# A decoder layer with 32 experts: expert 0's gather in two column pieces, its bias in the last quarter, and the first input chunk ahead of token tile 1

## The reference, cut to what matters

```python
h = rms_norm(x, norm1_w)                       # x: 256 tokens x 1024
proj = h @ w_in                                # 1024 x 3072: rq rk rv rg mq mk mv
ret  = retention(rotary(rq), rotary(rk), rv)   # 4 heads; group norm, times silu(rg)
moba = causal attention(rotary(mq), rotary(mk), mv)   # 8 heads of 64, one block of 256
x = x + concat(ret, moba) @ w_out
h2 = rms_norm(x, norm2_w)
logits = h2 @ w_router + b_router              # 32 experts, top 4, softmax over the chosen
for e in experts:                              # over the tokens that chose e
    u = h2[tok] @ w1[e] + b1[e]                # 1024 -> 2048: gate and linear halves
    y = clamped_swiglu(u) @ w2[e] + b2[e]      # 1024 -> 1024
    acc[tok] += y * gate
out = rms_norm(x + acc, final_norm_w)
```

## Time and profile before

| | before |
|---|---|
| median of 3 runs | 1040.47 us (1039.09 to 1041.36) |
| profiled execution, in all | 1039.17 us |
| its span, first to last instruction | 1037.3 us |
| TensorE matmuls busy | 1020.7 us, 98% of the span |
| VectorE busy | 245.4 us, 24% |
| ScalarE busy | 126.5 us, 12% |
| read from HBM | 422.78 MB, 409 GB/s over the span |
| granted TensorE clock | 0.997 of full |

### The profile page before, as it was taken

The page is one execution under the profiler, slowest core; times in us unless marked ns, Lnnn a source line. Parts: engine busy times, 40 slices in busy tenths (PEclk is TensorE's granted clock), DMA queues, the critical chain, the costliest instruction groups (busy, mean ns, idle before and its releaser), DMA issues.

```text
span 1037.3 us, 11270 instructions
## 1 busy us (share of the span) xinstructions
PE 1020.7 (98%) x4880; PEld 409.8 (40%) x4880; DVE 245.4 (24%) x610; ACT 126.5 (12%) x246; POOL 0.2 (0%) x4
## 2 busy tenths in 40 slices
PE   9999999999999999999999999999999999999996
PEld 8888433333333333333333333333333333333331
DVE  5776332111111111111111111111111111111111
ACT  2433120000000000000000000000000000000002
POOL 0000000000000000000000000000000000000000
PEclk9999999999999999999999999999999999999999
DMA  9983999999999999999999999999999999999995
GB/s 324 365 337 143 418 376 425 426 428 426 434 432 426 438 429 427 435 427 429 434 429 433 430 428 437 429 428 435 426 432 433 429 430 433 428 436 420 430 421 227
DMA packets 36104, 424.64 MB, mean 409 GB/s; under 512 B 3176, under 2 KB 16112, under 8 KB 19536
## 3 DMA queue, kind: packets, MB, share of 16 engines
q1 hardware_dynamic: 35744, 423.51, 97.0%
q10 hardware_dynamic: 304, 0.33, 0.1%
HBM read 422.78 MB, written 1.05 MB: 409 GB/s over the span
## 4 chain that ended last, share of the span: by engine, by line
PE 90%; DMA 7%; SPq 1%; DVE 0%; another core or an unknown queue 0%; issue 0%; ACT 0%; DVEq 0%
PE PS L1837 40%; PE PS L1860 19%; DMA ring<-in_w 7%; PE PS L1442 6%; PE PS L1806 5%; PE PS L1788 5%; PE PS L1685 3%; PE PS L1645 3%; PE PS L1895 2%; PE PS L1798 2%; PE PS L1411 1%; PE PS L1780 1%; SPq L543 1%; PE PS L1388 0%; PE PS L1968 0%; PE PS L1982 0%
## 5 line engine op out<-in xcount | busy, mean ns | idle before, releaser
L1837 PE MATMUL PS<-ring,work 128*64 128x512 f32 x1976 | 433.8, 596 | 6.0 <-DMA ring<-in_w 5.5
L1837 PEld LDWEIGHTS PS<-ring,work 128*64 128x64 f32 x1976 | 139.6, 137 | 277.2 <-issue 266.5
L1860 PE MATMUL PS<-ring,work 128*64 128x512 f32 x1024 | 227.9, 596 | 0.9 <-DMA ring<-in_w 0.8
L1860 PEld LDWEIGHTS PS<-ring,work 128*64 128x64 f32 x1024 | 72.0, 137 | 153.8 <-issue 148.9
L1300 DVE TENSOR_SCALAR work<-PS 128x512 f32<-128x512 f32 x32 | 22.1, 691 | 385.4 <-PE PS L1837 385.4
L841 ACT ACTIVATE work<-work 128x512 f32<-128x512 f32 x32 | 20.2, 631 | 523.5 <-DVE work L1300 523.5
L1265 DVE TENSOR_TENSOR work<-PS,n2w 128x512 f32<-128x512 f32 x30 | 20.7, 691 | 228.5 <-PE PS L1798 228.5
L1442 PE MATMUL PS<-ring 128*128 128x256 f32 x280 | 64.5, 382 | 0.0
L1806 PE MATMUL PS<-late,work 64*128 64x512 f32 x248 | 61.9, 616 | 0.0
L1788 PE MATMUL PS<-resid,work 128*64 128x512 f32 x248 | 58.5, 592 | 0.0
L1442 PEld LDWEIGHTS PS<-ring 128*128 128x128 f32 x280 | 51.7, 190 | 7.7 <-issue 1.4
(11 more groups left out here) (196 smaller groups left out, 453.2 us busy)
## 6 DMA issues: line engine op xcount, KB each, us to landing
ring<-in_w SPq DMA_DIRECT2D x72, 4096.0 KB, 34.8
ring<-in_w SPq DMA_DIRECT2D x35, 2048.0 KB, 13.5
ring<-in_w SPq DMA_DIRECT2D x22, 1024.0 KB, 8.4
ring<-in_w_in SPq DMA_DIRECT2D x11, 1024.0 KB, 12.1
ring<-in_w_out SPq DMA_DIRECT2D x4, 1024.0 KB, 11.1
ring<-in_w SPq DMA_DIRECT2D x6, 512.0 KB, 7.0
ring<-in_w_in SPq DMA_DIRECT2D x2, 512.0 KB, 5.8
work<-in_w SPq DMA_DIRECT2D x1, 768.0 KB, 8.2
```

The source lines that it names most:

```text
L1837: last = mm(bank(b0 + v)[64 * half:64 * half + 64, :], rows[:, c, :], turned_half(w[:, v * F:(v + 1) * F], half), start=(second and c == 0 ...
L1860: last = mm(out[64 * half:64 * half + 64, :], aT_n[:, c, 64 * h:64 * h + 64], ring[:, 2 * d + c // 2, cols:cols + BANK], start=(h == 0 and ...
```

## The change

- **Start.** The first half of `w_in`'s chunk 0 comes in two pieces (`WIN0_PARTS`, blocks 0 to 1 and 2 to 3), its second half is loaded ahead of x's tile 1 instead of behind it, and `project_first` does seven of tile 0's eight blocks before it transposes tile 1 (`X_TURN_AT`).
- **Projected columns.** `nat` is 1536 columns a tile instead of 3072: three areas of 512 that several chunks use one after the other (`NAT_COL`). With `mixT_moba` it fills slots 16 and 17 alone. Slot 18 and half of slot 19 are free.
- **Loads.** Three quarters of g 9 (`EARLY`, 1.5 MiB) are loaded right behind g 3, the last quarter once `w_in` is used up. The order of g 6, 8, 9, 11 changes. `moved_w` comes in one load of 1 MiB when the logits are done.
- **Expert 0's gather.** It is cut by columns into pieces `a` = 0 and 1 of 256 columns for each half of the partitions, in banks 4 and 7; rows go to `gx1`, outside `moved_w`. Each engine copies two pieces, four full 128 x 128 transposes take the place of the eight small ones, and `gh` is made in four parts, of which the first lets expert 0 begin.
- **Bias.** Expert 0's `b1` is added by the ordinary `bias` ahead of its last quarter (q = 3), its selector made by `make_bsel(0)` on VectorE behind the gather; `make_bsel(1)` moves behind `take_gather(1)`.

The diff, cut to its core:

```diff
-TURN0_BANK = (5, 3)
+ROWS0_BANK, TURN0_BANK = (4, 7), (5, 3)
...
+WIN0_PARTS, X_TURN_AT = [(0, 2), (2, C // 2)], C - 1
...
+AREA_A, AREA_B, AREA_C, NAT_COLS = 0, 512, 1024, 1536
+NAT_COL = [AREA_A, AREA_A + 256, AREA_B, AREA_B + 256, AREA_A, AREA_A + 256, AREA_B, AREA_B + 256,
+           AREA_C, AREA_C + 256, AREA_B, AREA_B + 256]
+NAT_V, NAT_RV, NAT_RG, NAT_RET, NAT_SIG = AREA_A, AREA_C, AREA_B, AREA_C, AREA_A
...
-FIRST_ORDER = [0, 1, 2, 3, 4, 5, 10, 11, 6, 8, 9, 7]
+FIRST_ORDER = [0, 1, 2, 3, 4, 5, 10, 9, 11, 8, 6, 7]
+EARLY, EARLY_COLS = 9, 3 * 1024
...
-        nat_flat = ring[:, HEAD_CHUNKS:HEAD_CHUNKS + 3, :].rearrange("p s n -> p (s n)")
-        nat = nat_flat.rearrange("p (t n) -> p t n", t=T)
-        mixT_moba = ring[:, HEAD_CHUNKS + 3, 0:4 * SEQ].rearrange("p (c n) -> p c n", c=4)
+        nat_flat = ring[:, HEAD_CHUNKS:HEAD_CHUNKS + 2, :].rearrange("p s n -> p (s n)")
+        nat = nat_flat[:, 0:T * NAT_COLS].rearrange("p (t n) -> p t n", t=T)
+        mixT_moba = nat_flat[:, T * NAT_COLS:].rearrange("p (c n) -> p c n", c=4)
...
-            load_win(0, 0, C // 2, win0_in)
+            for n, (c0, c1) in enumerate(WIN0_PARTS):
+                load_win(0, c0, c1, win0_in[n])
+            load_win(0, C // 2, C, head_full[0])
             sp.dma_start(resid[:, 1, :], x_v[:, 1, :]).then_inc(x_in[2], 16)
...
+            early_dst = ring[:, 2 * EARLY:2 * EARLY + 2, :].rearrange("p a n -> p (a n)")
+            early_src = w2_half(0, 1)
...
                 elif g == 8:
                     sp.wait_ge(retT_done, 2)
-                elif g == 9:
-                    sp.wait_ge(retT_done, 2)
                     sp.wait_ge(chunk_used, HEAD_CHUNKS - 2)
+                elif g == EARLY:
+                    sp.wait_ge(chunk_used, WIN_CHUNKS)
                 else:
                     sp.wait_ge(chunk_used, min(2 * g + 2, HEAD_CHUNKS))
...
                     sp.dma_start(ring[:, 2 * d + 1, :], w2_half(1, 1)[:, SLOT_COLS:]).then_inc(ahead_in, 16)
+                    sp.dma_start(early_dst[:, 0:EARLY_COLS], early_src[:, 0:EARLY_COLS]).then_inc(early_part_in, 16)
+                elif g == EARLY:
+                    sp.dma_start(early_dst[:, EARLY_COLS:], early_src[:, EARLY_COLS:]).then_inc(pair_full[EARLY], 16)
...
-            sp.dma_start(moved_w[:, BANK:], moved_src[:, BANK:]).then_inc(moved_in, 16)
-            sp.wait_ge(gather0_done, 2)
-            sp.dma_start(moved_w[:, 0:BANK], moved_src[:, 0:BANK]).then_inc(moved_end_in, 16)
+            sp.dma_start(moved_w, moved_src).then_inc(moved_in, 16)
...
-            act.wait_ge(rows0_done, 1)
-            nc.scalar.activation(gx[0:64, :], bank(4)[0:64, :], ACT.Copy).then_inc(rows0a_ready, 1)
+            for a in range(2):
+                act.wait_ge(rows0_done, a + 1)
+                nc.scalar.activation(gx1[0:64, a * SEQ:(a + 1) * SEQ], bank(ROWS0_BANK[a])[0:64, 0:SEQ],
+                                     ACT.Copy).then_inc(rows0a_ready, 1)
...
-            dve.wait_ge(rows0_done, 2)
-            nc.vector.tensor_copy(gx[64:P, :], bank(4)[64:P, :]).then_inc(rows0b_ready, 1)
-            take_gather0(0).then_inc(gh0_ready, 1)
-            take_gather0(1).then_inc(gh_ready, 1)
-            dve.wait_ge(bias_done, 1)
+            def take_rows0(a):
+                dve.wait_ge(rows0_done, a + 1)
+                nc.vector.tensor_copy(gx1[64:P, a * SEQ:(a + 1) * SEQ],
+                                      bank(ROWS0_BANK[a])[64:P, 0:SEQ]).then_inc(rows0b_ready, 1)
+            def take_gather0(half, a):
+                c = 4 * half + 2 * a
+                return nc.vector.tensor_tensor(gh[:, c:c + 2, :],
+                                               bank(TURN0_BANK[a])[:, 0:2 * P].rearrange("p (c h s) -> p h c s", c=2, h=2)[:, half],
+                                               n2w[:, c:c + 2].unsqueeze(2).broadcast_to([P, 2, SLOTS]), ALU.mult)
+            take_rows0(0)
+            take_rows0(1)
+            dve.wait_ge(gather0_done, 1)
+            take_gather0(0, 0).then_inc(gh0_ready, 1)
+            dve.wait_ge(gather0_done, 2)
+            take_gather0(0, 1).then_inc(gh0_ready, 1)
+            take_gather0(1, 0).then_inc(gh0_ready, 1)
+            take_gather0(1, 1).then_inc(gh_ready, 1)
+            make_bsel(0)
             make_pick(1)
             softmax(0)
             softmax(1)
             link(nc.vector.reduce_max(most[:, :], bank(2)[:, T * E:(T + 1) * E], AX.X))
             nc.vector.tensor_copy(most_i[:, :], most[0:1, :]).then_inc(most_ready, 1)
             take_gather(1)
+            dve.wait_ge(bias_done, 1)
+            make_bsel(1)
             run_experts(dve, expert_dve, 0)
             with dve.If(read["dve"] > SLOTS):
             def project_first():
...
-                pe.wait_ge(win0_in, 16)
                 pe.wait_ge(hT_ready, 1)
-                project_part(0, 0, 0, C // 2)
+                for n, (c0, c1) in enumerate(WIN0_PARTS):
+                    pe.wait_ge(win0_in[n], 16)
+                    project_part(0, 0, c0, c1)
+                pe.wait_ge(head_full[0], 16)
+                pe.wait_ge(hT_ready, 2)
+                project_part(0, 0, C // 2, X_TURN_AT)
                 for half in range(2):
                     transpose_x(1, half)
-                pe.wait_ge(head_full[0], 16)
-                pe.wait_ge(hT_ready, 2)
-                project_part(0, 0, C // 2, C)
+                project_part(0, 0, X_TURN_AT, C)
                 pe.wait_ge(hT_ready, 4)
                 project_part(0, 1, 0, C // 2)
                 pe.wait_ge(ones_ready, 1)
...
+            def gather0_rows(t, a):
+                for half in range(2):
+                    last = mm(bank(ROWS0_BANK[a])[64 * half:64 * half + 64, 0:SEQ], pick[:, t, :],
+                              resid[:, t, half * BANK + a * SEQ:half * BANK + (a + 1) * SEQ],
+                              start=(t == 0), stop=(t == T - 1))
+                return last
+            def turn_rows0(a):
+                gx_v = gx1.rearrange("p (i s) -> p s i", s=DEAL)
+                for s in range(2):
+                    last = nc.tensor.transpose(bank(TURN0_BANK[a])[:, s * P:(s + 1) * P], gx_v[:, 2 * a + s, :], ident)
                 last.then_inc(gather0_done, 1)
...
             pe.wait_ge(pick0_ready, 1)
-            for half in range(2):
-                gather0_rows(0, half)
+            for a in range(2):
+                gather0_rows(0, a)
             pe.wait_ge(member_ready, T)
             mm(bank(2)[:, E:2 * E], ones_w[:, :], member[:, 0, :], start=True, stop=False)
             mm(bank(2)[:, E:2 * E], before_w[:, :], member[:, 1, :], start=False, stop=True)
             mm(bank(2)[:, 2 * E:3 * E], ones_w[:, :], member[:, 0, :], start=True, stop=False)
             mm(bank(2)[:, 2 * E:3 * E], ones_w[:, :], member[:, 1, :], start=False, stop=True).then_inc(prefix_done, 1)
-            pe.wait_ge(late_in, 48)
-            pe.wait_ge(bsel_ready, 1)
-            bias_half(0, bsel0)
             pe.wait_ge(pick_ready, 1)
-            for half in range(2):
-                gather0_rows(1, half).then_inc(rows0_done, 1)
-            bias_half(1, bsel0).then_inc(bias_done, 1)
-            pe.wait_ge(rows0a_ready, 1)
-            turn_rows0(0)
-            pe.wait_ge(rows0b_ready, 1)
-            turn_rows0(1)
+            for a in range(2):
+                gather0_rows(1, a).then_inc(rows0_done, 1)
+            pe.wait_ge(rows0a_ready, 2)
+            pe.wait_ge(rows0b_ready, 2)
+            for a in range(2):
+                turn_rows0(a)
             def put_transposes(n, out):
...
-                    if first and q == W1_CHUNKS // 2:
+                    if first and q < W1_CHUNKS - 1:
+                        pe.wait_ge(gh0_ready, q + 1)
+                    if first and q == W1_CHUNKS - 1:
                         pe.wait_ge(gh_ready, 1)
+                        pe.wait_ge(late_in, 48)
+                        bias(0, 0, False)
                     for c in (2 * q, 2 * q + 1):
                         moved = first and q == MOVED and c % 2 == 1
...
+                if isinstance(r, int) and g == EARLY:
+                    pe.wait_ge(early_part_in, 16)
...
-                    pe.wait_ge(gh0_ready, n + 1)
```

More of the change, by code:

```diff
@@ L266, in layer_kernel @@
         retw = ring[:, HEAD_CHUNKS + 6, 1536:2048]
[L267 removed]
+        ret = nat[:, :, NAT_RET:NAT_RET + 512]
         h2T = work[:, 0:2048].rearrange("p (t c n) -> p t c n", t=T, c=C)
@@ L282, in layer_kernel @@
         bsel = work[0:2 * E, 1152:1216]
-        bsel0 = work[0:2 * E, 896:960]
         g_sb = work[:, 1280:1792]
@@ L296, in layer_kernel @@
         scr = sb("scr", [P, 256])
-        gsig = nat[:, :, MK:MK + 512]
+        gsig = nat[:, :, NAT_SIG:NAT_SIG + 512]
         gatesT = scr[2 * E:3 * E, 0:SEQ]
@@ L313, in layer_kernel @@
         moved_in = sem("moved_in")
-        moved_end_in = sem("moved_end_in")
+        early_part_in = sem("early_part_in")
         ahead_in = sem("ahead_in")
```

(19 more changed lines are left out.)

27 lines of the change are left out of this document (7 added, 20 removed).

## The result

| | before | after |
|---|---|---|
| median of 22 runs each, same chip | 1040.07 us (1038.45 to 1041.36) | 1041.2 us (1039.6 to 1043.17) |
| ratio to before | | 1.0014, 95% interval 1.0008 to 1.002 |
| profiled execution, in all | 1039.17 us | 1040.01 us |
| its span | 1037.3 us | 1038.1 us |

The time went up by 1.5 us by the ratio (1.1 us by the medians, 0.84 us between the two profiled executions). That is less than the 0.2% that was called "no change", but its interval lies clear of 1, and the forecast had named the other sign (-0.14 us). So the median lies in the forecast's range, but the direction and the sum were wrong.

The account below looks back on a forecast made before the run. Weight transfers, held by TensorE's slot releases, bound the kernel. The stream could come 0.97 us earlier, but TensorE 0.66 us later less 0.8 us slack left -0.14 us: 1040.3 us, range 1038.2 to 1042.2 us (its own 1038.6 to 1041.9).

Parts of the forecast that it names:

- What bounds the kernel: Whole span: the weight transfers end it plus a fixed tail; after 140 us each transfer needs a slot TensorE releases.
- The slack: Queue at 248.25 us: the stream can come forward 0.8 us (0.04 to 1.59) before it waits for TensorE.
- my own sum: At 248.25 us: TensorE 0.7 - 1.06 + 1.02 = 0.66 us later; with 0.8 us to spare, the end moves -0.14 us.
- The head: Kernel start, near 12 us: TensorE waits for tile 1's scaling, 0.5 us, plus an unhidden weight load, 0.2 us: 0.7 us later.
- Rival (c): Start: pieces ahead of tile 1 don't overlap, tile 1 lands at 14.6 us; +4.2 us, 1044.7 us; chance 0.06.
- The gather: Placement to expert 0, 136 to 140 us: two column pieces start expert 0 1.06 us earlier (0.7 to 1.3).
- The bias: Expert 0's last quarter: eight records nothing hides, making later releases 1.02 us later (0.9 to 1.1).
- The loads: Before 140 us: the early 1.5 MiB fill a hole worth nothing itself; 0.61 us less remains to do behind 140 us.
- Rival (a): Early 1.5 MiB count in full, releases never hold the stream: 3.68 us earlier, 1036.8 us; chance 0.09.
- Rival (b): First chunk costs nothing, room at 248.25 us at its upper bound, 144 to 150 us may heal: 1039.5 to 1038.4 us; chance 0.10.
- The chances: Whole run: 0.77 for a change within 0.2%, 0.14 for faster by more, 0.09 for slower by more.
- Slower: Whole run over 0.2% longer: non-overlapping pieces at the start plus a tail of the forecast's own; chance 0.09.

Follow-up runs that it names:

- twice_expert3: Kernel before with the matmuls of expert 3's gather issued twice, 1.72 us more TensorE work near 200 us: 1040.68 us against 1039.58, ratio 1.0011.
- the dose at 147 us: Kernel before with the matmuls of expert 1's gather issued twice, 1.72 us more TensorE work: 1041.27 us against 1039.58, ratio 1.0017.
- changed_old_head: Changed kernel with the old start, other parts kept: 1040.72 us against 1040.09 for the kernel before, ratio 1.001.
- changed_again: Changed kernel measured a second time, unaltered, beside its variants: 1040.31 us against 1040.09 for the kernel before, ratio 1.0008.
- loads_alone: Kernel before with only the shared columns, the early 1.5 MiB and the new load order: 1039.12 us against 1039.61, ratio 0.9996.
- gather_bias_alone: Kernel before with only the gather in pieces, bias in expert 0's last quarter, moved chunk in one load: 1040.34 us against 1039.61, ratio 1.001.
- twice_expert8: Kernel before with the matmuls of expert 8's gather issued twice, 1.72 us more TensorE work near 337 us: 1039.32 us against 1039.58, ratio 0.9994.

## Why the prediction was wrong, step by step

**What bounds the kernel: right, and too coarse.** The stream does end the span, and releases after expert 0's start move it. But I read one place, 248.25 us, for a contact that lasts from 150 us on.

**The slack, 0.8 us (bounds 0.04 and 1.59): the step that failed.** It stood for how far the stream may come forward before TensorE's releases hold it. I took the time over the bytes of one load (3.88 us) and subtracted that of a load into an empty queue. Two things are wrong with it. The place: the stream is held from 150 us on, and what it loses there comes back at no later point. The contact isn't over at 197 us either: in `twice_expert3`, with its dose at 202 us, the load issued at 219.34 us lands at 228.7 us, 1.4 us later than the one at 217.45 us in the kernel before. And the measure: the load at 193.52 us has 9.3 - 4.9 = 4.4 us over its bytes in the kernel before, more than the 3.88 us at 248.25 us, and yet with the dose at 147 us it lands later by about what its issue is late, though by my measure it would have 0.6 to 2.1 us to spare. So toward later releases in this stretch I put the slack at about 0; the dose's time, 1.7 us for 1.72 us, says the same within 0.9 us either way. With 0 in its place my own sum gives +0.66 us. That has the right sign, but is below the interval of the ratio (+0.8 to +2.1 us) and under half of its middle; it is near the 0.84 us between the two profiled executions.

**The head, +0.7 us: right in kind, too large.** The gap came: VectorE's scaling stands in the chain. The matmul with the scales at 13.83 us is 0.50 us later than in the trace of before. But that trace had luck: in it the first half of chunk 0 was there before TensorE wanted it. In the eight further traces with the old start that matmul begins between 13.49 and 14.21 us, in `changed_old_head` behind this landing:

```profile
1.65 5.95 DMA ring<-in_w_in
7.61 0.04 issue
7.65 1.99 PE PS L1425 x8
```

The nine old starts have a mean of 13.69 us, the four new ones (13.77, 13.83, 14.20, 14.21) of 14.00 us. The head costs about 0.3 us, which the comparison of `changed_old_head` with `changed_again` can't resolve. Rival (c), pieces that don't overlap, is refuted by tile 1's own landing in the changed kernel, issued at 3.15 us:

```profile
DMA to landing us min/median/max: 6.6/6.6/6.6
```

It is there at 9.75 us (10.0 us was forecast, 14.6 us was the rival's), and its transposes begin by 10.02 us. The last three of the four loads, issued at 2.12, 2.63 and 3.15 us, are there at 7.1, 8.4 and 9.75 us, some 1.3 us apart, little more than the 1.2 us that 512 KB take at 427 GB/s. The fixed part of about 2 us, which the prediction takes from the Trainium skill, "DMA: Bandwidth & Descriptors", section "Anatomy of one DMA — SWDGE (gpsimd) path", is given there for transfers that GpSimd issues; these come from the sync engine, and no such part is paid here piece by piece.

**The gather, -1.06 us: 0.80 us.** The copies came out as forecast, 138.52 - 136.90 = 1.62 us behind placement against 1.59. What is missing lies in the steps between the engines: TensorE starts 0.14 us behind VectorE, twice, where I had 0.05 us, after the earlier trace rows, which show the other direction, VectorE behind TensorE (in the kernel before, TensorE began expert 0 only 0.04 us behind VectorE, at 139.90 us; why it is 0.14 us now, no run shows); and the two transposes with the step behind them take 0.52 us instead of 0.48. With the product's 0.30 us for 0.28 these make the rest.

**The bias, +1.02 us: exact.** Put together, 0.5 - 0.8 + 1.02 = 0.72 us; the issue at 248.98 us is 0.73 us late, forecast 0.66. With the head's mean price of 0.3 us in place of 0.5 it would be some 0.5 us.

**The loads, nothing at the end: right.** But the 0.97 us by which the stream was to come forward (0.61 us of it the missing piece) is there only at 150 us (0.45 MiB, 1.1 us) and gone by 175 us. Rival (a), 3.68 us faster, is refuted: 1.5 MiB of lead at 100 us are 0.45 MiB at 150 us, where slots are short, and `loads_alone` isn't faster by more than its interval. Rival (b) is refuted too; its wish for the thin stretch at 144 to 150 us came true (400 against 349 GB/s) and brought nothing, since 150 to 200 us gave it back.

**The chances.** No change of over 0.2% had 0.77, and that came; the median of 1041.2 us lies in the range. "Slower" had too little weight inside that case: with the slack's lower bound, 0.04 us, the sum was already +0.62 us, and I took the middle of an interval whose one end was the thin queue's own reading. The forecast's own range, 1038.6 to 1041.9 us, doesn't follow from what it names either: 1039.09 - 0.93 and 1041.36 + 0.62 give 1038.2 to 1042.0 us. The median is inside both.

**Still open.** One for one, 0.5 to 0.7 us of lateness account for half or less of the 1.5 us that the first measurement has by its ratio; the second has 0.8 us. In `gather_bias_alone` too the ratio gives 1.0 us for releases 0.4 us later. In the trace the stream fell back 0.90 MiB (2.2 us) between 150 and 195 us while TensorE was 0.73 us late and the stream had been 1.1 us ahead, some 0.4 us more than lateness accounts for. The dose at 147 us did so too: 0.93 MiB or 2.3 us behind at 200 us, with releases 1.9 us late. No run separates a further cause from the scatter between executions: `twice_expert8` is 0.2 MiB (0.4 us) behind the kernel before at 200 us, long before its dose.

## What to carry to other kernels

Where one engine frees the buffers that a stream of loads fills, look at the stretch with the shortest times from issue to landing over many loads, not at one load at a convenient place, and price work moved into that stretch at its full length; take the slack as zero until a dose has shown some. Bytes loaded earlier were worth nothing here, since the stream waited for slots later. Compare landings over several executions: one and the same code differed by 1 us at 203 us. Before moving work out of a short wait into a dense stream, put it into another wait of the same engine: the bias cost TensorE 1.02 us in the stream and 0.34 us behind the copies.

## What the hardware showed that I had not expected

- A queue short of work shows as slower more than as idle engines: 405 GB/s at a DMA share of 1.00 for 50 us, against 424 GB/s at 1.01 in the kernel before and 418 GB/s at 1.01 in `twice_expert8`. The dose at 147 us gives the same 405 GB/s at 1.00.
- The load of the first 512 KB at the kernel's start, issued at 1.65 us, lands after 5.5 to 6.0 us in four executions, while in others TensorE, ready for it at 7.0 to 7.1 us, did not wait. In two more the second half of the chunk was what TensorE waited for. With the same start, the matmul with the scales moves by up to 0.9 us from one kernel's trace to the next (13.33 to 14.21 us), as much as the edits priced here.
- The response is one-sided by the middle values: 1.72 us more of TensorE's work at 147 us costs 1.7 us (0.8 to 2.6), 2.6 us less from 147 us on gives 0.4 us (at most 1.2).
